# Feed-forward up projections of a two-block model kernel: rounded activations and remainder streamed side by side, 512 columns per weight load

## Reference

```
def swiglu_half_step(h, g, w1, w3, w2):
    u = rmsnorm(h, g)
    return h + FFN_HALF * ((jax.nn.silu(u @ w1) * (u @ w3)) @ w2)
...
D_MODEL = 1024   SEQ = 256   D_FF = 2816   FFN_HALF = 0.5
```

## Time and profile before

| | |
|---|---|
| median of 3 runs | 2665.18 us (2663.08 to 2665.87) |
| span of the profiled execution | 2662.5 us |
| TensorE matmul busy | 2355.1 us, 88% of the span |
| TensorE weight load busy | 2097.6 us, 79% |
| VectorE busy | 1597.9 us, 60% |
| ScalarE busy | 1019.2 us, 38% |
| mean granted TensorE clock | 0.947 of full speed |

### The profile page before, as it was taken

How to read it: one execution, slowest core, us unless ns; L and a number is a source line. 1 busy time by engine, 2 the same in 40 slices (tenths; PEclk the granted TensorE clock), 3 DMA queues, 4 the chain that set the end, 5 groups by cost and what they waited for, 6 DMA issues and landing times.

```text
span 2662.5 us, 43491 instructions
## 1 busy us (share of the span) xinstructions
PE 2355.1 (88%) x15136; PEld 2097.6 (79%) x15136; DVE 1597.9 (60%) x2836; ACT 1019.2 (38%) x1469; POOL 98.5 (4%) x81
## 2 busy tenths in 40 slices
PE   6997888999799868998767787996899999899998
PEld 6996876899699747997667645886779998789998
DVE  4555776655455445555534344888876667666665
ACT  4334444434343344444311334223334443344443
POOL 0000000000000000000000000003300003300000
PEclk9998888999899999998797988998999999999999
DMA  5553333455555334554100102431166651266664
GB/s 183 187 191 129 127 134 120 157 183 179 185 195 183 126 93 137 181 187 145 53 0 0 41 23 89 149 126 63 42 189 187 187 175 56 70 199 187 188 186 138
DMA packets 101765, 357.58 MB, mean 134 GB/s; under 512 B 11136, under 2 KB 17168, under 8 KB 100944
## 3 DMA queue, kind: packets, MB, share of 16 engines
q1 hardware_dynamic: 100224, 346.34, 39.6%
q0 software_dynamic: 1488, 10.54, 1.1%
HBM read 352.59 MB, written 4.25 MB: 134 GB/s over the span
## 4 chain that ended last, share of the span: by engine, by line
PE 74%; DVE 10%; ACT 5%; DMA 5%; issue 3%; DVEq 3%; ACTq 1%; SPq 0%
PE bank L315 56%; PE bank L341 6%; PE bank L1219 3%; PE bank L1920 2%; DVE w_lo L295 2%; DMA ring<-in_expert_v 2%; DVEq L2118 1%; DMA ring<-in_ssm_in 1%; ACT w_hi L290 1%; DVE arena L2116 1%; DMA ring<-in_expert_u 1%; PE bank L1263 1%; DMA ring<-in_w 1%; PE bank L1199 1%; PE bank L1552 1%
## 5 line engine op out<-in xcount | busy, mean ns | idle before, releaser
L295 DVE TENSOR_TENSOR w_lo<-ring,w_hi 128x1024 fp32r<-128x1024 f32 x580 | 700.9, 1223 | 464.4 <-ACT w_hi L290 462.9
L290 ACT ACTIVATE w_hi<-ring 128x1024 fp32r<-128x1024 f32 x580 | 603.7, 1056 | 676.2 <-PE bank L315 543.5
L315 PE MATMUL bank<-u_hi,w_hi 128*128 128x256 f32 x2656 | 760.3, 286 | 14.1 <-DVE arena L783 7.2
L315 PE MATMUL bank<-u_lo,w_hi 128*128 128x256 f32 x2656 | 756.4, 285 | 0.0
L315 PE MATMUL bank<-u_hi,w_lo 128*128 128x256 f32 x2656 | 755.9, 285 | 0.0
L315 PEld LDWEIGHTS bank<-u_hi,w_hi 128*128 128x128 f32 x2656 | 514.7, 194 | 26.9 <-issue 16.3
L315 PEld LDWEIGHTS bank<-u_lo,w_hi 128*128 128x128 f32 x2656 | 514.3, 194 | 7.5 <-issue 0.5
L315 PEld LDWEIGHTS bank<-u_hi,w_lo 128*128 128x128 f32 x2656 | 514.1, 194 | 0.0
L315 PE MATMUL bank<-w_hi,x_hi 128*128 128x512 f32 x992 | 393.2, 396 | 19.6 <-DVE x_lo L2089 7.8
L315 PE MATMUL bank<-w_lo,x_hi 128*128 128x512 f32 x992 | 390.6, 394 | 0.0
L315 PE MATMUL bank<-w_hi,x_lo 128*128 128x512 f32 x992 | 388.1, 391 | 0.0
(11 more groups left out here) (310 smaller groups left out, 1947.0 us busy)
## 6 DMA issues: line engine op xcount, KB each, us to landing
ring<-in_w SPq DMA_DIRECT2D x264, 512.0 KB, 3.4
ring<-in_expert_u SPq DMA_DIRECT2D x128, 512.0 KB, 3.6
ring<-in_expert_v SPq DMA_DIRECT2D x128, 512.0 KB, 4.2
ring<-in_ssm_in SPq DMA_DIRECT2D x40, 512.0 KB, 4.5
ring<-in_ssm_out SPq DMA_DIRECT2D x16, 512.0 KB, 3.3
ring<-in_w_o SPq DMA_DIRECT2D x16, 512.0 KB, 4.1
ring<-in_w_pq SPq DMA_DIRECT2D x16, 512.0 KB, 5.8
ring<-in_rwkv_in SPq DMA_DIRECT2D x14, 512.0 KB, 3.8
```

The source lines that it names most:

```text
L290: act.activation(w_hi[slot][:, :], ring[slot][:, :], ACT.Copy).then_inc(hi_made[slot], 1)
L295: dve.tensor_tensor(w_lo[slot][:, :], ring[slot][:, :], w_hi[slot][:, :].bitcast(F32), ALU.subtract).then_inc(freed[slot], 1)
L315: mm = pe.matmul(out, left[a], right[b], start=start and n == 0, stop=stop and n == 2, skip_group_check=True)
```

## The change

The two activation tensors become one, `u_both`, in which a chunk's 256 rounded columns and its 256 remainder columns lie side by side; `u_hi` and `u_lo` are views of it. In the feed-forward stages `project_wide` replaces `project_split`: with `w_hi` loaded once it streams all 512 columns into one full PSUM bank, and then with `w_lo` the 256 rounded columns into the bank's left half. The right half then holds w_hi·u_lo and has to be added to the left. Each `up` so fills two banks instead of one. ScalarE copies the two right halves to SBUF (`small`), VectorE adds each to its left half (`whole`), and `silu` and `gate` read the sums from SBUF. In both engines' orders `silu(b)` and `gate(b)` now stand behind the first `make_hi` and the first `make_lo` of the half step.

```diff
-        u_hi, u_lo = sb("u_hi", [P, DC, T], F32R), sb("u_lo", [P, DC, T], F32R)
+        u_both = sb("u_both", [P, DC, 2, T], F32R)
+        u_hi, u_lo = u_both[:, :, 0, :], u_both[:, :, 1, :]
...
+        def project_wide(pe, b, slot, stage, i, nth=0, first=False):
+            multiplied(pe, slot, stage, i, nth)
+            for c in range(DC):
+                cols = slice(c * P, (c + 1) * P)
+                if first and c % (DC // 2) == 0:
+                    u_split_ready(pe, stage, 2 + c // 2)
+                pe.matmul(b[:, :], w_hi[slot][:, cols], u_both[:, c, :, :].rearrange("p a t -> p (a t)"),
+                          start=c == 0, stop=False, skip_group_check=True)
+                mm = pe.matmul(b[:, 0:T], w_lo[slot][:, cols], u_hi[:, c, :], start=False, stop=c == DC - 1,
+                               skip_group_check=True)
             return mm.then_inc(split_read[slot], 1)
...
+        up_buf = area(18 * D, 2, 2, T)
+        small_buf = area(19 * D, 2, 2, T)
...
                 for n in range(2):
-                    project_split(pe, UP[b][:, n * T:(n + 1) * T], *ffn_tile(n, k, i, b), first=first and n == 0)
+                    project_wide(pe, ROT[2 * b + n], *ffn_tile(n, k, i, b), first=first and n == 0)
...
         def ffn_scalar(act, k):
+            def small(b, i):
+                for n in range(2):
+                    split_done(act, *ffn_tile(n, k, i, b))
+                    act.activation(small_buf[:, b, n, :], ROT[2 * b + n][:, T:2 * T],
+                                   ACT.Copy).then_inc(S("small_ready"), 1)
+
             def silu(b, i):
-                split_done(act, *ffn_tile(1, k, i, b))
-                act.activation(silu_buf[:, b, :], UP[b][:, 0:T], ACT.Silu).then_inc(S("silu_ready"), 1)
+                act.wait_ge(S("up_ready"), FC * ffn_no[f"ffn{k}"] + 2 * i + b + 1)
+                act.activation(silu_buf[:, b, :], up_buf[:, b, 0, :], ACT.Silu).then_inc(S("silu_ready"), 1)
...
                 for b in range(2):
+                    small(b, i)
+                    kind, *at = ffn_next(k, i, b)[0]
+                    make_hi(act, *ffn_tile(kind, k, *at))
                     silu(b, i)
-                    for kind, *at in ffn_next(k, i, b):
+                    for kind, *at in ffn_next(k, i, b)[1:]:
                         make_hi(act, *ffn_tile(kind, k, *at))
+            small(0, FC // 2 - 1)
+            make_hi(act, *ffn_tile(2, k, FC // 2 - 1, 1))
             silu(0, FC // 2 - 1)
-            make_hi(act, *ffn_tile(2, k, FC // 2 - 1, 1))
+            small(1, FC // 2 - 1)
             silu(1, FC // 2 - 1)
...
+            def whole(b, i):
+
+                for n in range(2):
+                    dve.wait_ge(S("small_ready"), 2 * FC * ffn_no[stage] + 4 * i + 2 * b + n + 1)
+                    ins = dve.tensor_tensor(up_buf[:, b, n, :], ROT[2 * b + n][:, 0:T], small_buf[:, b, n, :], ALU.add)
+                ins.then_inc(S("up_ready"), 1)
+
             def gate(b, i):
...
-                dve.tensor_tensor(x_hi[:, b, :], silu_buf[:, b, :], UP[b][:, T:2 * T], ALU.mult)
-                dve.tensor_tensor(hid_buf[:, b, :], silu_buf[:, b, :], UP[b][:, T:2 * T], ALU.mult)
+                dve.tensor_tensor(x_hi[:, b, :], silu_buf[:, b, :], up_buf[:, b, 1, :], ALU.mult)
+                dve.tensor_tensor(hid_buf[:, b, :], silu_buf[:, b, :], up_buf[:, b, 1, :], ALU.mult)
...
                 for b in range(2):
+                    whole(b, i)
+                    kind, *at = ffn_next(k, i, b)[0]
+                    make_lo(dve, *ffn_tile(kind, k, *at))
                     gate(b, i)
-                    for kind, *at in ffn_next(k, i, b):
+                    for kind, *at in ffn_next(k, i, b)[1:]:
                         make_lo(dve, *ffn_tile(kind, k, *at))
```

More of the change, by code:

```diff
@@ L326, in project_split @@
                             c == 0, c == DC - 1)
+            return mm.then_inc(split_read[slot], 1)
+        def project_wide(pe, b, slot, stage, i, nth=0, first=False):
[8 more added lines that the diff above has]
+                               skip_group_check=True)
             return mm.then_inc(split_read[slot], 1)
@@ L563, in ffn_vector @@
                 for b in range(2):
+                    whole(b, i)
+                    kind, *at = ffn_next(k, i, b)[0]
+                    make_lo(dve, *ffn_tile(kind, k, *at))
                     gate(b, i)
-                    for kind, *at in ffn_next(k, i, b):
+                    for kind, *at in ffn_next(k, i, b)[1:]:
                         make_lo(dve, *ffn_tile(kind, k, *at))
+            whole(0, FC // 2 - 1)
+            make_lo(dve, *ffn_tile(2, k, FC // 2 - 1, 1))
             gate(0, FC // 2 - 1)
-            make_lo(dve, *ffn_tile(2, k, FC // 2 - 1, 1))
+            whole(1, FC // 2 - 1)
             gate(1, FC // 2 - 1)
```

## The result

The changed kernel takes 2764.34 us (median of 4 runs, 2760.57 to 2767.70) against 2664.13 us (4 runs, 2659.91 to 2665.87) in the same comparison: ratio 1.0376, 95% interval 1.0361 to 1.0392. A second comparison (the eighth experiment) gave 2758.59 against 2663.86 us, ratio 1.0354 (1.0337 to 1.0370). The forecast was 2746 us in a range of 2722 to 2770: slower, as forecast, by 3.5 to 3.8% where 3.0% were expected.

A forecast was written before the change was run, and what follows sets the result against it. TensorE alone was taken to set the time. Loops +76.8 us, half steps outside them -1.5 and stage starts +5.3 gave +80.6 us, so 2746 us, 3.0% slower, range 2722 to 2770.

The forecast's parts named there:

- The mechanism and its sign: Feed-forward loops: moved gate makes TensorE wait 1.16 us ahead of each down; slower, chance 0.93.
- The chain: From the first half's end through make_hi, make_lo and gate to down's matmul: 3.94 us, against 2.78 us of cover.
- The saving per product: Each half of up: one 512 and one 256 pass replace three of 256, 12 ns a chunk, 0.096 us per product.
- the table of waits: TensorE's profiled waits ahead of down, released by x_lo: 80 of some 0.9 us, 71 us, 76 with stage starts.
- half steps: In the four feed-forward loops: 9.46 us each against 8.50, 0.96 us more, 76.8 us over 80.
- The 8 half steps outside the loops: No slot-0 step ahead of silu there, so each keeps 2 x 0.096 us: -1.5 us.
- The starts of the stages: Second slot-0 make_hi waits for its load: 1.7, 0.1, 3.5 and 0.1 us late in the four stages, 5.3 in all.
- My rival of the clock: Waits ahead of down lower TensorE's mean clock to 0.85: 80 us more, about 2825 us; chance 0.05.

The follow-up runs named there:

- the eighth experiment: The changed kernel run again unaltered for a second profiled execution: 2758.59 us against 2663.86 us for the kernel before, ratio 1.0354.
- Experiment 3: The kernel before, with only silu and gate moved behind the first make_hi and make_lo in the loops: 2752.88 us, ratio 1.0345.
- experiment 1: The changed kernel with silu and gate put back ahead of the slot-0 pair: 2663.89 us against 2662.54, ratio 1.0003.
- experiment 7: The changed kernel with gate put back ahead of the first make_lo, silu left behind the first make_hi: 2695.97 us, ratio 1.0116.
- experiment 2: The kernel before with u_hi and u_lo as views of one tensor, nothing else: 2665.82 us against 2662.54, ratio 1.0009.
- experiment 6: The kernel before with 56 VectorE and 39 ScalarE drains at the start of the fourth feed-forward stage: 2670.09 us, ratio 1.0020.
- experiment 5: The kernel of experiment 1 with 8 VectorE and 25 ScalarE drains at the start of the fourth feed-forward stage: 2661.16 us, ratio 0.9989.
- 10: The kernel of experiment 1 with only 8 VectorE drains at the start of the fourth feed-forward stage: ratio 1.0003.
- 9: The kernel of experiment 2 with the wide product but no copies or additions, silu and gate reading left halves, orders of before: 2662.24 us, ratio 0.9990.
- experiment 11: The kernel of experiment 1 with only 25 ScalarE drains at the start of the fourth feed-forward stage: ratio 0.9989.

## Why the prediction was right, and by how much it was off

**The mechanism and its sign were right.** The step that decided was that `gate(b)`, moved behind the slot-0 pair, can't begin before the first half of the next `up` is over. Experiment 3 has only that step and loses 3.45%; experiment 1 has all of the change but that step and loses nothing; experiment 7 takes one link out of the chain and two thirds of the loss go.

**The chain.** Forecast 3.94 us, read 3.91 (0.25 + 1.10 + 1.14 + 1.25 + 0.06 + 0.11). Each link was taken from a row of before, and each came back within 0.03 us.

**The saving per product was taken too large; two fifths of it did not come.** I took 12 ns a chunk. A half takes 63.30 - 60.48 = 2.82 us, 353 ns a chunk, so it is 7 ns. The 512 and 256 passes together need 5 ns more than each alone at the pace of its width. The isolated pace of the Trainium skill's page "TensorE: Matmul & The Clock Gate" (section "Back-to-back issue gap"), by which merging two passes of 256 would save 2.5 ns, lies on the other side of what was measured. By the same 0.04 us the second half covers more, 2.83 us, which is most of why the table of waits shows 71.9 us and not 76. The cost of my error is 0.04 us in the first half: half steps of 9.51, 9.54, 9.48 and 9.45 us in the four stages, 9.50 in the mean, where I had 9.46. 80 x (9.50 - 8.50) = 80 us instead of 76.8. The 8 half steps outside the loops gave back 8 x 2 x 0.06 = 0.9 us and not 1.5.

**The starts of the stages.** In the first stage I had 1.7 us more. There the second slot-0 `make_hi` came at 34.98, after 31.86 for the one before it: 34.98 - (31.86 + 2.82) = 0.3 us late. Its load landed sooner than in the kernel before; why, no run shows. In the third stage I had 3.5 us more, and the `make_hi` was late as forecast. The rows of both stages:

```profile
31.86 1.06 ACT L291 ACTIVATE w_hi<-ring 128x1024 fp32r<-128x1024 f32 x1 [1.71 <-PE bank L338]
...
34.98 1.06 ACT L291 ACTIVATE w_hi<-ring 128x1024 fp32r<-128x1024 f32 x1 [1.51 <-DMA ring<-in_w]
...
764.95 1.06 ACT L291 ACTIVATE w_hi<-ring 128x1024 fp32r<-128x1024 f32 x1 [1.77 <-PE bank L338]
...
771.77 1.06 ACT L291 ACTIVATE w_hi<-ring 128x1024 fp32r<-128x1024 f32 x1 [5.21 <-DMA ring<-in_w]
...
775.38 0.79 PE L316 MATMUL bank<-w_hi,x_hi 128*128 128x512 f32 x1 [4.88 <-DVE x_lo L590]
```

771.77 - (764.95 + 2.82) = 4.0 us late. The wait that came of it, 4.9 us, ended at 775.38, and the clock fell in it, which I had not priced: 770 to 772 has a mean granted clock of 1.00, the stretch 772 to 777, over half of it waiting, has 0.54, and 777 to 782, with TensorE busy throughout, has 0.78 (rows above). From this `x_lo` to the next (774.83 to 786.12) it is 11.3 us, 1.8 more than in the loop; I put the clock's price at these 2 us. The second profiled execution has the same: a wait of 5.0 us, then a clock of 0.53 and 0.85, and 11.1 us to the next `x_lo`. The part grew by 25.7 us where the second and fourth stages grew by 21.2 and 19.4. The four stages in sum: 80 for the loops, 4.7 for late loads (0.3, 0.2, 4.0, 0.2), 2 for the clock and 0.9 given back make 86 us. The four parts grew by 86, where 80.6 were forecast. My rival of the clock was wrong for the loops, where 0.8 us of idle in every 9.5 leave it at 1.00, and right at this one place.

**The step that failed is one that I never wrote down**: that stages that aren't changed keep their time. They account for some 10 of the 13 to 18 us by which the forecast was low. The layout isn't the cause (experiment 2), nor is it that they begin 80 us later (experiment 3). Added instructions are a part of it: drains alone made the kernel before 0.2% slower (experiment 6). The number of instructions on VectorE goes with the waits in the expert stage: 34.1 to 34.4 us in all five profiles with the original number, 37.3 to 37.4 us in the five with 48 more, 35.8 to 36.4 us in the three with 56 more (experiments 5, 6, 10). In the sum of the last two parts the five profiles with the original VectorE and ScalarE counts (before twice, experiments 2, 3, 9) lie at 1424 to 1429 us, and seven of the eight others at 1433 to 1437, the eighth (experiment 11) at 1426. Part is chance of the execution, some 3 us here.

The traces show one more thing that differs, TensorE's clock. In RWKV to output projection its mean is 0.85 or 0.86 in the five profiles with the original counts; it is 0.84 in experiment 6 (424.0 us), experiments 1 and 10 and the first profile of the changed kernel (425.1 us), and 0.86 in experiment 11 (414.1 us). By an estimate from these numbers, 0.01 of the mean clock over 417 us is at most 4 us. But the second profile of the changed kernel and experiment 5 have 0.85 and take 421.6 and 422.9 us, and experiment 7 has 0.86 and takes 419.6. So it isn't the clock alone, and no run separates a lower clock that costs time from a lower clock that follows from longer waits. That it is the place of the later code among the instructions, and not something else about the added ones, is argued and not shown. What rule joins the number of instructions to the time stays open, and the cause of these 10 us with it.

## What to carry to other kernels

When an instruction moves in an engine's order past one that waits for another engine, the price is read from that other wait: time from its release through everything up to the consumer, less what covers it. Here it was 3.9 us against 2.8, 80 times over: 1.1 us lost per half step for a gain of 0.06 us per product. A new wait ahead of an instruction isn't by itself a reason to move it: `silu` kept in its place waited 1.6 us on an idle ScalarE and delayed nothing. And an expected gain of 0.3 to 0.4% (10 us here) is of the size of what parts that nobody changed can take back: experiment 1 got 7 to 9 us from the feed-forward parts and nothing in all.

## What was not expected of the hardware

- A pass of 512 columns followed by one of 256 with another weight takes 353 ns for the two, where rows of passes of one width take 228 and 120 ns each, 348 together.
- 56 drains on VectorE and 39 on ScalarE in idle time made the kernel before slower by a ratio of 1.0020 (1.0011 to 1.0030). In the profile a later, untouched part takes 424.0 us, where it takes 414.2 to 418.9 us in the five profiles without added instructions.
- One wait of 4.9 us cost TensorE's clock: 0.54 in the stretch of 5 us in which it ended and 0.78 in the next, while the waits of some 0.8 us ahead of the other `down` passes left it at 1.00 in 45 to 213 us.
